# Output projection and final LayerNorm run from inside the attention loop, with the query blocks outermost

## The chip, the cores and the metric

The kernel runs on all 8 cores of one Trainium2 chip, one batch element per core, and every core executes the same program. The metric is the device time in microseconds of the slowest core. A core has a matrix engine (PE, with its weight loads listed as PEld), a vector engine (DVE), a scalar engine (ACT), GpSimd (POOL) and SyncE (SP). Each takes its instructions in the order of the program and stops at the first one whose semaphores are not there yet.

## The reference, cut to what matters

The layer gates two mixers, one of them softmax attention with 8 heads over 2048 latent queries and 2304 keys (256 context tokens and 2048 latents), concatenates them, projects to 1024 columns, and ends with a residual LayerNorm:

```
q  = rms_norm(q_a) @ w_qb              # (2048, 8 heads, 64+32), the last 32 rotated
kv = rms_norm(kv_a) @ w_kvb            # (2304, 8 heads, 64 key + 64 value)
p  = softmax((qn.kn + qr.kr) * scale)  # per head, 2048 x 2304
y_a = (p @ v) * silu(z_a)
y   = concat([y_a, y_b]) @ w_out
h_new = layer_norm(ALPHA * h + gate * y) * ln_g + ln_b      # h = layer_norm(x) * ln_in_g + ln_in_b
```

## The kernel before

The program is a list of operations, written in order. `P.add` (line 55) gives each a list of tile names that it reads and writes, works out from these names which earlier operations it has to wait for, and `flush` (line 126 on) puts each on its engine's queue with the waits. So the order in which the Python code emits operations is the order of every engine, and a tile name is all that decides a wait. A PSUM name (`psA0`, `psC`, ...) counts as written by whoever touches it, so matmuls into one bank and the reader of that bank alternate strictly.

The stages, in order: input LayerNorm and modulation; the mLSTM mixer, which fills `ycatT` rows 4 to 7; the attention inputs (`qnT`, `kvnT`, `szaT`, the rotary half of `Kh`); the attention loop (lines 882 to 975); and the output stage (lines 976 to 1064). `P.barrier()` separates them. `uT`, the modulated input, has no reader after the attention inputs.

**Attention loop.** `mainloop(h, pro)` takes one head and runs over four blocks of 512 queries; one (head, block) is called an iteration here, and there are 32. An iteration has 21 steps. Step s (below 18) issues the score matmul QK(s) into `psA[s % 3]` and its exponential on ACT into `PT[s % 4]`; from step 3 on it also issues PV(s-3), which adds to `psO` or `psE`. Two closures are left for the next iteration: `ep1` at its step 3 (reciprocal of the softmax sum by Ln and Exp on ACT, then a CAST and a subtraction on DVE into `rhl`) and `ep2` at its step 8 (two matmuls into `psB`, then `gg` and `ycatT` on DVE). `RECIP` and `RSQRT` are both Ln followed by Exp.

**Prologue.** `prologue(h + 1)` is a generator that makes the next head's keys, values and queries in 12 slots, one at each of steps 4, 10 and 16: five slots K0 to K4 (one matmul into `psC`, one CAST to `Kh`; K0 is 256 wide, the others 512), three slots V0 to V2 (8, 8 and 2 matmuls of 64 columns into `psD`, one CAST to `Vh`), four slots Q (two matmuls into `psC`, two into `psD`, four DVE operations). All evacuations are on DVE. Heads alternate between two `Kh`, `Vh` and `Qh` buffers.

**Output stage.** It starts after the barrier: `gate_bc` is built in 8 rounds of DVE, PE, ACT; four rows are loaded and broadcast to `rowsb`; `wout` is scaled by the gate in 8 DVE operations; then 16 tiles of 128 rows follow. A tile is 20 matmuls of 512 columns in two banks out of six (`bankset`), the residual add and statistics, RSQRT, two ACT normalisations, four DVE operations and a store. `xin` has three buffers, `pre` and `xo` two, and `stage1(lt + 1)`, the input side of the next tile, is issued ahead of tile lt's matmuls.

Helper lines: every matmul is recorded at line 234, ACT with a bias at 240, ACT without at 238, tensor_tensor at 249, tensor_scalar at 244, copies at 257 (ACT) and 259 (DVE).

Of the kernel before, what the change touches and what calls it, by code (L numbers as in the profile page):

```python
# [6 lines left out]
F32 = mybir.dt.float32  # L7
# [193 lines left out]
def build_nc(stage=99, dbg=None):  # L201
# [25 lines left out]
    def sbx(stack, name, shape, dt=F32):  # L227
        return stack.enter_context(nc.sbuf_tensor(name, list(shape), dt))
# [530 lines left out]
    if stage >= 3:  # L759
# [119 lines left out]
        MSET("dve", Vh[1][:], 0.0, w=[("Vh", 1)])  # L879
        MSET("dve", Vh[0][:, :, 64:65], 1.0, w=[("Vh", 0)])  # L880
        MSET("dve", Vh[1][:, :, 0:1], 1.0, w=[("Vh", 1)])
        def prologue(h):
            hb_ = h % 2
            voff = 0 if hb_ == 0 else 64
            for bi, (t0, N) in enumerate(blocks):
# [3 lines left out]
            for g0 in range(0, NT, 8):  # L889
# [4 lines left out]
                       r=["wkv", "kvnT"], w=["psD"])  # L894
                CP("dve", Vh[hb_][:, g0:g0 + nt_, voff:voff + 64], pv[:, 0:nt_, :], r=["psD"], w=[("Vh", hb_)])
                yield
            for qb in range(4):
                qs = slice(qb * 512, (qb + 1) * 512)
                for c in range(2):
                    MM(psC[0:96, :], wqA[:, c, h, :], qnT[:, c, qs], start=(c == 0), stop=(c == 1),  # L900
                       r=["wqA", ("qnT", c)], w=["psC"])
                for c in range(2):
                    MM(psD[0:96, :], wqB[:, c, h, :], qnT[:, c, qs], start=(c == 0), stop=(c == 1),
                       r=["wqB", ("qnT", c)], w=["psD"])
                CP("dve", Qh[hb_][0:64, qs], psC[0:64, :], r=["psC"], w=[("Qh", hb_, qb)])
                TT("dve", tmp_th[64:96, :], psC[64:96, :], rope[64:96, 0, qs], ALU.mult, r=["psC", "rope"],
                   w=["tmp_th"])
                TT("dve", tmp_zz[64:96, :], psD[64:96, :], rope[64:96, 1, qs], ALU.mult, r=["psD", "rope"],
                   w=["tmp_zz"])
                TT("dve", Qh[hb_][64:96, qs], tmp_th[64:96, :], tmp_zz[64:96, :], ALU.add,  # L910
                   r=["tmp_th", "tmp_zz"], w=[("Qh", hb_, qb)])
                yield

        pending = []

        def mainloop(h, pro):
            hb_ = h % 2
            M = 65 if hb_ == 0 else 128
            pd = 64 if hb_ == 0 else 0
            r0 = 0 if hb_ == 0 else 64  # L920
            for qb in range(4):
                qs = slice(qb * 512, (qb + 1) * 512)
                ob = (h * 4 + qb) % 2
                pso = psO if ob == 0 else psE
                pok = "psO" if ob == 0 else "psE"
                SK = 3
                for step in range(NT + SK):
# [6 lines left out]
                    if step >= SK:  # L934
                        kt = step - SK
                        MM(pso[0:M, :], Vh[hb_][:, kt, 0:M], PT[kt % 4][:], start=(kt == 0), stop=(kt == NT - 1),
                           r=[("Vh", hb_), ("PT", kt % 4)], w=[pok])
                    if pro is not None and step % 6 == 4:
                        next(pro, None)
                    if step == 3 and pending:  # L940
                        pending.pop(0)()
                    if step == 8 and pending:
# [33 lines left out]
    if stage >= 4:
        so = ExitStack()
        gate_bc = sbx(so, "gate_bc", [128, D])
        dg = sbx(so, "dg", [128, 128])
        for c in range(8):  # L980
            TS("dve", dg[:], ident_f[:], ada[:, 16 + c, 0:1], None, ALU.mult, r=["ident_f", ("ada", 2, 0)], w=["dg"])
            MM(psA[c % 2][:, 0:128], ones_f[:], dg[:], r=["ones_f", "dg"], w=["psA%d" % (c % 2)])
            CP("act", gate_bc[:, c * 128:(c + 1) * 128], psA[c % 2][:, 0:128], r=["psA%d" % (c % 2)], w=[("gate_bc", c)])
        rowsb = sbx(so, "rowsb", [128, 4, D])
        for a in range(4):
            DMA("sp", rowsb[:, a, :], rows_d[a:a + 1, :].partition_broadcast(128), w=[("rowsb", a)])
        xin = [sbx(so, "xin%d" % i, [128, D]) for i in range(3)]
        NPRE = 2
        for lt in range(NPRE):
            DMA("sp", xin[lt % 3][:], x_d[lt * 128:(lt + 1) * 128, :], w=[("xin", lt % 3)])  # L990
        for a in range(2):
            TS("dve", rowsb[:, a, :], rowsb[:, a, :], ALPHA, None, ALU.mult, r=[("rowsb", a)], w=[("rowsb", a)])
        for k in range(8):
            TT("dve", wout[:, k, :], wout[:, k, :], gate_bc[:], ALU.mult, r=["wout", "gate_bc"], w=[("wout", k)])
        bhl = sbx(so, "bhl", [1, 2, D], BF16)
        CP("dve", bhl[0:1, 0, :], rowsb[0:1, 1, :], r=[("rowsb", 1)], w=["bhl"])
        TT("dve", bhl[0:1, 1, :], rowsb[0:1, 1, :], bhl[0:1, 0, :], ALU.subtract, r=[("rowsb", 1), "bhl"], w=["bhl"])
        nmr = sbx(so, "nmr", [128, NT])
        STT("dve", nmr[:], stats[:, :, 0], -1.0, stats[:, :, 1], ALU.mult, ALU.mult, r=["stats"], w=["nmr"])
        nmo = sbx(so, "nmo", [128, 1])  # L1000
        xo = [sbx(so, "xo%d" % i, [128, D]) for i in range(2)]
        pre = [sbx(so, "pre%d" % i, [128, D]) for i in range(2)]
        st6o = sbx(so, "st6o", [128, 2, 6])
        mvo = sbx(so, "mvo", [128, 2])

        def prefetch(lt):
            if lt + NPRE < 16:
                nb = (lt + NPRE) % 3
                DMA("sp", xin[nb][:], x_d[(lt + NPRE) * 128:(lt + NPRE + 1) * 128, :], w=[("xin", nb)])

        def stage1(lt):
            xb = lt % 3
            ti = lt + 2
            ACT(xin[xb][:], xin[xb][:], AF.Identity, r=[("xin", xb), "nmr"], w=[("xin", xb)],
                scale=stats[:, ti, 1:2], bias=nmr[:, ti:ti + 1])
            TT("dve", xin[xb][:], xin[xb][:], rowsb[:, 0, :], ALU.mult, r=[("xin", xb), ("rowsb", 0)],
               w=[("xin", xb)])

        prefetch(0)
        stage1(0)  # L1020
        for lt in range(16):
            b = lt % 2
            xb = lt % 3
            cs = slice(lt * 128, (lt + 1) * 128)
            if lt + 1 < 16:
                stage1(lt + 1)
            bankset = [((psA[0], "psA0"), (psA[1], "psA1")), ((psA[2], "psA2"), (psO, "psO")),
                       ((psC, "psC"), (psD, "psD"))][lt % 3]
            for hf in range(2):
                hs = slice(hf * 512, (hf + 1) * 512)  # L1030
                pt_, pk_ = bankset[hf]
                for k in range(8):
                    MM(pt_[:], ycatT[:, k, cs], wout[:, k, hs], start=(k == 0), stop=False,
                       r=["ycatT", ("wout", k)], w=[pk_])
                for a in range(2):
                    MM(pt_[:], ones_b[0:1, :], bhl[0:1, a, hs], start=False, stop=(a == 1),
                       r=["ones_b", "bhl"], w=[pk_])
            for hf in range(2):
                hs = slice(hf * 512, (hf + 1) * 512)
                pt_, pk_ = bankset[hf]  # L1040
                TT("dve", pre[b][:, hs], pt_[:], xin[xb][:, hs], ALU.add, r=[pk_, ("xin", xb)],
                   w=[("pre", b, hf)])
                P.add("dve", lambda e, b=b, hf=hf, hs=hs: e.bn_stats(out=st6o[:, hf, :], in_=pre[b][:, hs]),  # L1043
                      r=[("pre", b, hf)], w=[("st6o", hf)])
            P.add("dve", lambda e: e.bn_aggr(out=mvo[:], in_=st6o[:]), r=["st6o"], w=["mvo"])  # L1045
            RSQRT(mvo[:, 1:2], mvo[:, 1:2], LN_EPS, r=["mvo"], w=["mvo"])
            STT("dve", nmo[:], mvo[:, 0:1], -1.0, mvo[:, 1:2], ALU.mult, ALU.mult, r=["mvo"], w=["nmo"])
            if lt + 1 < 16:
                prefetch(lt + 1)
            for hf in range(2):  # L1050
                hs = slice(hf * 512, (hf + 1) * 512)
                ACT(pre[b][:, hs], pre[b][:, hs], AF.Identity, r=[("pre", b, hf), "mvo", "nmo"], w=[("pre", b, hf)],
                    scale=mvo[:, 1:2], bias=nmo[:])
            for hf in range(2):
                hs = slice(hf * 512, (hf + 1) * 512)
                TT("dve", pre[b][:, hs], pre[b][:, hs], rowsb[:, 2, hs], ALU.mult, r=[("pre", b, hf), ("rowsb", 2)],
                   w=[("pre", b, hf)])
                TT("dve", xo[b][:, hs], pre[b][:, hs], rowsb[:, 3, hs], ALU.add, r=[("pre", b, hf), ("rowsb", 3)],
                   w=[("xo", b, hf)])
            DMA("pool", out_d[cs, :], xo[b][:], r=[("xo", b)], w=[("outd", lt)])  # L1060
        P.add("sp", lambda e: e.nop(), r=["outd"])
        P.barrier()
        so.close()
# [66 lines left out]
```

How the kernel before makes its waits and increments, by code:

```python
        def run(e):  # L146
            eng = eobj[e]
            seen = self.seen[e]
            for i in per[e]:
                op = ops[i]
                need = {}
                for d in op["deps"]:
                    dop = ops[d]
                    if (not dop["dma"]) and dop["eng"] == "pe" and e == "pe" and not op["dma"]:
                        continue
                    sem = dop["sem"]
                    key = id(sem)
                    if dop["val"] > need.get(key, (None, 0))[1]:
                        need[key] = (sem, dop["val"])
                for key, (sem, val) in need.items():
                    if seen.get(key, 0) >= val:
                        continue
                    eng.wait_ge(sem, val)
                    self.nwaits += 1
                    seen[key] = val
                ins = op["fn"](eng)
                if op["dma"]:
                    ins.then_inc(op["sem"], 16)
                elif op["sig"]:
                    ins.then_inc(op["sem"], 1)
                op["fn"] = None
```

## Time and profile before

| | us |
|---|---|
| median of the runs shown (1448.73 and 1452.82) | 1450.77 |
| the profiled execution | 1458.9 |
| its span on the slowest core (core 4) | 1457.1 |
| spans of the other cores | 1439.7 to 1456.9 |
| PE / DVE / ACT busy in the span | 906.9 / 753.7 / 842.5 |

The span runs from a core's first to its last instruction; the execution's own time is 1.8 us more. Busy time is the time in which an engine had an instruction under way. Matmuls overlap, so the busy time of one (about 0.38 us for 512 columns) is longer than the distance between two.

### The profile page before, as it was taken

To read this page: it belongs to the slowest core of one execution; us is meant where nothing else is said; L and a number is where in the kernel's file an instruction comes from. 1 tells how busy PE (TensorE), PEld (TensorE's weight loads), DVE (VectorE), ACT (ScalarE), POOL (GpSimd) and SP (SyncE) were. 2 spreads that over 40 slices of the span, in tenths; PEclk is the share of its full clock that TensorE was granted. 3 is DMA by queue.
4 is the path that set the end of the run, shared out by engine and by line. 5 is a ranking of instruction groups with operands and counts; after the bars stand their busy time and mean duration, and the time that the engine had idled before them with its cause. 6 is when DMAs were issued, how large, how long until landed. Compare 5 with 4: busy or idle time off the path is not lost. (4 is left out here: it accounts for less than half of the span.)

```text
span 1457.1 us, 18426 instructions; the slowest of 8 cores (1439.7 to 1457.1 us)
## 1 busy us (share of the span) xinstructions
PE 906.9 (62%) x5007; PEld 431.7 (30%) x5061; DVE 753.7 (52%) x1378; ACT 842.5 (58%) x1688; POOL 25.5 (2%) x40
## 2 busy tenths in 40 slices
PE   0113286466676554544229668888999988859770
PEld 0112142255543332323114323223333333213220
DVE  0267224456634655657625654455355345267776
ACT  0266324466656776667524428888877887813332
POOL 0000200000000000000000000000000000000000
PEclk9999996667687777776559959999888899957765
DMA  9742200000000000000040030000000000033331
GB/s 237 197 143 87 61 1 1 1 1 1 2 1 1 1 1 1 1 1 0 1 155 1 0 58 1 1 1 1 1 1 1 1 1 1 1 102 117 116 115 71
DMA packets 20308, 54.14 MB, mean 37 GB/s; under 512 B 4656, under 2 KB 6704, under 8 KB 20144
## 3 DMA queue, kind: packets, MB, share of 16 engines
q1 hardware_dynamic: 13232, 40.32, 8.9%
q0 software_dynamic: 6976, 12.63, 3.5%
q8 instruction: 45, 0.74, 0.2%
q14 instruction: 55, 0.45, 0.1%
HBM read 48.80 MB, written 8.39 MB: 39 GB/s over the span
## 5 line engine op out<-in xcount | busy, mean ns | idle before, releaser
L238 ACT ACTIVATE PT<-psA 128x512 bf16<-128x512 f32 x576 | 300.9, 601 | 71.4 <-PE psA L234 69.4
L234 PE MATMUL psA<-Qh,Kh 96*128 96x512 bf16 x576 | 226.7, 412 | 38.3 <-ACT PT L238 36.9
L234 PE MATMUL psO<-PT,Vh 128*65 128x512 bf16 (+1 forms) x280 | 111.7, 417 | 3.0 <-ACT PT L238 2.1
L234 PE MATMUL psE<-PT,Vh 128*65 128x512 bf16 (+1 forms) x281 | 109.4, 406 | 1.9 <-ACT PT L238 0.7
L234 PEld LDWEIGHTS psA<-Qh,Kh 96*128 96x128 bf16 x576 | 58.4, 101 | 169.6 <-issue 150.8
L259 DVE CAST rhl<-rden 1x512 bf16<-1x512 f32 x32 | 13.3, 416 | 131.6 <-ACT rden L238 131.6
L234 PE MATMUL psA<-wout,ycatT 128*128 128x512 bf16 x132 | 44.4, 486 | 17.8 <-DVE pre L249 10.0
L240 ACT ACTIVATE mvo<-mvo 128x1 f32<-128x1 f32 x16 | 3.2, 203 | 87.9 <-DVE mvo L1045 87.9
L234 PE MATMUL psA<-S0m,Vp 128*128 128x128 bf16 x128 | 26.1, 280 | 42.4 <-DVE S0m L249 42.4
L234 PE MATMUL psA<-uT,watt 128*128 128x512 bf16 (+3 forms) x127 | 28.7, 384 | 35.5 <-ACT wqA L257 35.5
L234 PE MATMUL psB<-scc,wadab 128*128 128x2 bf16 x192 | 5.5, 165 | 71.5 <-ACT wadab L257 68.0
L367 DVE BATCH_NORM_STATS2 st<-xt 128x6 f32<-128x512 f32 x36 | 23.0, 681 | 50.0 <-DMA xt<-ctx 41.3
L234 PE MATMUL psA<-uT,wxm 128*128 128x512 bf16 (+1 forms) x157 | 33.0, 374 | 23.9 <-DVE wxm L259 23.5
L238 ACT ACT_TABLE_LOAD x15 | 19.2, 1283 | 47.6 <-PE psA L234 38.8
L234 PE MATMUL psC<-Qd,KT 128*128 128x128 bf16 x128 | 15.9, 264 | 45.9 <-ACT KT L257 33.9
L252 DVE SCALAR_TENSOR_TENSOR state<-state,Ebc,dU 128x129 f32<-128x129 f32 x144 | 41.5, 348 | 4.9 <-ACT dU L238 4.4
L240 ACT ACT_TABLE_LOAD x11 | 14.1, 1283 | 50.0 <-DVE stats L259 43.8
L234 PE MATMUL psC<-xcT,wbd 128*128 128x128 bf16 (+2 forms) x133 | 17.7, 264 | 40.3 <-ACT wcol L238 37.8
L238 ACT ACTIVATE absd<-absd 128x512 f32<-128x512 f32 x64 | 40.3, 630 | 3.1
L234 PEld LDWEIGHTS psO<-PT,Vh 128*65 128x65 bf16 (+1 forms) x288 | 32.2, 112 | 30.5 <-issue 24.6
L259 DVE CAST Kh<-psC 64x512 bf16<-64x512 f32 (+1 forms) x40 | 25.1, 628 | 30.0 <-PE psC L234 29.3
L234 PEld LDWEIGHTS psE<-PT,Vh 128*65 128x65 bf16 (+1 forms) x288 | 31.4, 109 | 30.3 <-issue 23.6
(316 smaller groups left out, 2159.9 us busy)
## 6 DMA issues: line engine op xcount, KB each, us to landing
wada<-w_ada SPq DMA_DIRECT2D x3, 4096.0 KB, 22.1
xt<-x SPq DMA_DIRECT2D x16, 512.0 KB, 3.6
xin<-x SPq DMA_DIRECT2D x16, 512.0 KB, 4.5
out<-xo POOLq DMA_DIRECT2D x16, 512.0 KB, 3.0
win<-w_in SPq DMA_DIRECT2D x2, 1856.0 KB, 7.3
wxm<-w_in SPq DMA_DIRECT2D x2, 1024.0 KB, 7.4
wout<-w_out POOLq DMA_DIRECT2D x1, 2048.0 KB, 14.5
rowsb<-rows SPq DMA_DIRECT2D x4, 512.0 KB, 7.2
```

Source lines behind the costliest of these rows:

```text
L234: P.add("pe", lambda e: e.matmul(out, lhsT=lhsT, rhs=rhs, start=start, stop=stop), r=r, w=w)
L238: P.add("act", lambda e: e.activation(out=out, in_=in_, func=func, scale=scale), r=r, w=w)
L240: P.add("act", lambda e: e.activation(out=out, in_=in_, func=func, scale=scale, bias=bias), r=r, w=w)
L252: P.add(eng, lambda e: e.scalar_tensor_tensor(out=out, in0=in0, scalar=scalar, in1=in1, op0=op0, op1=op1), r=r, w=w)
L259: P.add(eng, lambda e: e.tensor_copy(out=out, in_=in_), r=r, w=w)
L367: P.add("dve", lambda e, b=b, hh=hh, s2=s2: e.bn_stats(out=st6[s2][:, hh, :], in_=xt[b][:, hh * 512:(hh + 1) * 512]), r=[("xt", b)], w=[(" ...
```

## The change

The attention loop is turned inside out: the outer loop runs over the four query blocks (`sb`), the inner over the 8 heads, and `mainloop` covers one block. The prologue of the next (head, block) makes all keys and values of that head again, and one query block. It has 9 slots, K0 to K4, V0 to V2 and one Q, taken at every even step.

The output stage becomes a generator, `outgen`. From the second block on (`allowed` is 0 in the first) it is advanced at steps 1, 4, 7, 10, 13, 16 and 19. It has 8 slots for the scaling of `wout` and then 17 for each tile; the projection is cut into quarters of 256 columns, which alternate between `psC` and `psD`. `pre` and `xo` have one buffer each instead of two, and all its large buffers lie in the memory of `uT`. What is left of it after the last iteration is run through at the end. The set-up (`gate_bc`, `rowsb`, `bhl`) stands ahead of the first prologue. The matmuls of the output read `("ycatT", 0)`, which covers every head and block.

```diff
-        def prologue(h):
+        def prologue(h, sb):
 ...
-            for qb in range(4):
+            for qb in range(sb * QSB, (sb + 1) * QSB):
 ...
-        def mainloop(h, pro):
+        def mainloop(h, sb, pro, og):
 ...
+            allowed = sb * TPS
-            for qb in range(4):
+            for qb in range(sb * QSB, (sb + 1) * QSB):
 ...
-                    if pro is not None and step % 6 == 4:
+                    if pro is not None and step % 2 == 0:
                         next(pro, None)
+                    if og is not None and step % 3 == 1 and out_state["tile"] < allowed:
+                        next(og, None)
 ...
+        def outgen():
+            for k in range(8):
+                TT("dve", wout[:, k, :], wout[:, k, :], gate_bc, ALU.mult, r=[("wout", k), "pre1"], w=[("wout", k)])
+                yield
+            for lt in range(16):
+                out_state["tile"] = lt
+                yield
...
+                for q in range(4):
+                    qs_ = slice(q * 256, (q + 1) * 256)
+                    pt_, pk_ = (psC, "psC") if q % 2 == 0 else (psD, "psD")
+                    for k in range(8):
+                        MM(pt_[:, 0:256], ycatT[:, k, cs], wout[:, k, qs_], start=(k == 0), stop=False,
+                           r=[("ycatT", 0) if k < 4 else ("ycatT", 1, lt), ("wout", k)], w=[pk_])
+                    for a in range(2):
+                        MM(pt_[:, 0:256], ones_b[0:1, :], bhl[0:1, a, qs_], start=False, stop=(a == 1),
+                           r=["ones_b", "bhl"], w=[pk_])
+                    TT("dve", pre1[:, qs_], pt_[:, 0:256], xin[xb][:, qs_], ALU.add, r=[pk_, ("xin", xb)],
+                       w=[("pre1", q)])
+                    yield
...
-        for _ in prologue(0):
+        og = outgen()
+        for _ in prologue(0, 0):
             pass
-        for h in range(8):
-            pro = prologue(h + 1) if h < 7 else None
-            mainloop(h, pro)
+        for sb in range(NSB):
+            for h in range(8):
+                if h < 7:
+                    pro = prologue(h + 1, sb)
+                elif sb + 1 < NSB:
+                    pro = prologue(0, sb + 1)
+                else:
+                    pro = None
+                mainloop(h, sb, pro, og)
...
         while pending:
             pending.pop(0)()
+        for _ in og:
+            pass
```

The 17 slots of a tile: one that only sets the tile's number; ACT and DVE on each half of `xin` (4); the four quarters (4); statistics (1); RSQRT (1); `nmo` (1); two ACT normalisations (2); two pairs of DVE operations of 512 columns (2); the store (1).

## Rows read from the trace of the kernel before

**Rows 1.** Spans and mean granted clock, two of the eight cores
```profile
core 0: 1445.1 us, clock 0.838
core 4: 1457.1 us, clock 0.801
```

**Rows 2.** Stage windows, core 4: PE, PEld, DVE, ACT, POOL busy (count), PEclk, DMA, GB/s
```profile
836.60:861.40 24.80, 11.40 (x39) 4.14 (x40) 17.10 (x25) 0.00 (x0) 0.90 (x1) 0.50 0.50 85
861.40:1273.40 412.00, 367.80 (x1473) 129.60 (x1486) 185.59 (x296) 336.04 (x639) 0.00 (x0) 0.89 0.00 1
1303.60:1457.10 153.50, 102.26 (x306) 29.99 (x312) 108.46 (x176) 49.01 (x80) 8.57 (x16) 0.67 0.28 100
```

**Rows 3.** Instruction groups by form, 780 to 1250 us: busy us, mean ns, idle before
```profile
L238 ACT ACTIVATE PT<-psA 128x512 bf16<-128x512 f32 x540 | 282.4, 601 | 68.6 <-PE psA L234 66.6 <-PE psO L234 0.9
...
L259 DVE CAST Kh<-psC 64x512 bf16<-64x512 f32 x32 | 21.8, 680 | 27.2 <-PE psC L234 26.6
...
L259 DVE CAST Vh<-psD 128x512 bf16<-128x512 f32 x16 | 11.0, 687 | 18.5 <-PE psD L234 18.3
...
L234 PE MATMUL psD<-wkv,kvnT 128*128 128x64 bf16 x144 | 9.0, 203 | 2.1 <-DVE Vh L259 2.1
```

**Rows 4.** Timeline of an iteration of the last head, no prologue: start, us, instruction
```profile
1238.60 0.81 PE L234 MATMUL psA<-Qh,Kh 96*128 96x512 bf16 x3
1239.13 2.06 ACT L238 ACTIVATE PT<-psA 128x512 bf16<-128x512 f32 x4 [0.89 <-PE psA L234]
...
1242.45 0.41 DVE L259 CAST rhl<-rden 1x512 bf16<-1x512 f32 x1 [9.01 <-ACT rden L238]
1242.96 0.68 DVE L249 TENSOR_TENSOR rhl<-rden,rhl 1x512 bf16<-1x512 f32 x1
...
1249.92 0.81 PE L234 MATMUL psA<-Qh,Kh 96*128 96x512 bf16 x3
```

**Rows 5.** Timeline of two key slots, at step 4 (K0) and step 10 (K1)
```profile
1176.67 0.30 PE L234 MATMUL psC<-kvnT,wkv 128*64 128x256 bf16 x1
...
1179.46 0.42 DVE L259 CAST Kh<-psC 64x256 bf16<-64x256 f32 x1
...
1181.26 0.40 PE L234 MATMUL psC<-kvnT,wkv 128*64 128x512 bf16 x1
...
1181.99 0.68 DVE L259 CAST Kh<-psC 64x512 bf16<-64x512 f32 x1
```

**Rows 6.** Timeline of a query slot at step 16 and the next iteration's start
```profile
1104.46 0.70 PE L234 MATMUL psC<-qnT,wqA 128*96 128x512 bf16 x2
...
1105.27 0.68 DVE L259 CAST Qh<-psC 64x512 bf16<-64x512 f32 x1 [2.88 <-PE psC L234]
...
1107.04 0.96 PE L234 MATMUL psA<-Qh,Kh 96*128 96x512 bf16 x3
...
1107.45 0.68 DVE L249 TENSOR_TENSOR Qh<-tmp_th,tmp_zz 32x512 bf16<-32x512 f32 x1
```

**Rows 7.** Timeline of the first prologue, before the loop
```profile
841.67 0.42 DVE L259 CAST Kh<-psC 64x256 bf16<-64x256 f32 x1
...
854.52 0.68 DVE L249 TENSOR_TENSOR Qh<-tmp_th,tmp_zz 32x512 bf16<-32x512 f32 x1
...
861.47 1.49 PE L234 MATMUL psA<-Qh,Kh 96*128 96x512 bf16 x3
```

**Rows 8.** Timeline of the output stage's opening
```profile
1279.52 1.77 SPq L273 DMA_DIRECT2D rowsb<-rows  x4
1279.58 0.29 DVE L244 TENSOR_SCALAR dg<-ident_f,ada 128x128 f32<-128x128 f32 x1 [0.70 <-PEq L173]
...
1289.59 1.29 DVE L244 TENSOR_SCALAR rowsb<-rowsb 128x1024 f32<-128x1024 f32 x2
...
1291.07 10.53 DVE L249 TENSOR_TENSOR wout<-wout,gate_bc 128x1024 bf16<-128x1024 bf16 x8 [0.19 <-ACT gate_bc L257]
```

**Rows 9.** Instruction groups by form, 1245 to 1457 us
```profile
L234 PE MATMUL psA<-wout,ycatT 128*128 128x512 bf16 x132 | 44.4, 486 | 17.8 <-DVE pre L249 10.0 <-DVE wout L249 7.6 <-issue 0.2
L240 ACT ACTIVATE pre<-pre,nmo,mvo 128x512 f32<-128x512 f32 x32 | 24.3, 806 | 6.5 <-DVE nmo L252 6.5
```

**Rows 10.** Chain that ended last: the normalisation of tiles 0 and 15
```profile
1312.06 0.82 ACT pre L240
...
1447.14 0.82 ACT pre L240
```

More of the change, by code:

```diff
@@ L881, in build_nc @@
         MSET("dve", Vh[1][:, :, 0:1], 1.0, w=[("Vh", 1)])
-        def prologue(h):
+        NSB = 4
+        QSB = 4 // NSB
+        TPS = 16 // NSB
+        uTf = uT[:].rearrange("p c t -> p (c t)").bitcast(F32)
+        rowsb = uTf[:, 0:4096].rearrange("p (a n) -> p a n", n=D)
+        xin = [uTf[:, 4096 + i * 1024:4096 + (i + 1) * 1024] for i in range(3)]
+        xo1 = uTf[:, 7168:8192]
+        pre1 = uTf[:, 8192:9216]
+        gate_bc = pre1
+        dg = sbx(sa, "dg", [128, 128])
+        bhl = sbx(sa, "bhl", [1, 2, D], BF16)
@@ new lines, in build_nc @@
+        nmr = sbx(sa, "nmr", [128, NT])
+        nmo = sbx(sa, "nmo", [128, 1])
+        st6o = sbx(sa, "st6o", [128, 2, 6])
+        mvo = sbx(sa, "mvo", [128, 2])
+        NPRE = 2
+        for a in range(4):
+            DMA("sp", rowsb[:, a, :], rows_d[a:a + 1, :].partition_broadcast(128), w=[("rowsb", a)])
+        for lt in range(NPRE):
+            DMA("sp", xin[lt % 3], x_d[lt * 128:(lt + 1) * 128, :], w=[("xin", lt % 3)])
+        for a in range(2):
+            TS("dve", rowsb[:, a, :], rowsb[:, a, :], ALPHA, None, ALU.mult, r=[("rowsb", a)], w=[("rowsb", a)])
@@ new lines, in build_nc @@
+        CP("dve", bhl[0:1, 0, :], rowsb[0:1, 1, :], r=[("rowsb", 1)], w=["bhl"])
+        TT("dve", bhl[0:1, 1, :], rowsb[0:1, 1, :], bhl[0:1, 0, :], ALU.subtract, r=[("rowsb", 1), "bhl"], w=["bhl"])
+        STT("dve", nmr[:], stats[:, :, 0], -1.0, stats[:, :, 1], ALU.mult, ALU.mult, r=["stats"], w=["nmr"])
+        for c in range(8):
+            TS("dve", dg[:], ident_f[:], ada[:, 16 + c, 0:1], None, ALU.mult, r=["ident_f", ("ada", 2, 0)], w=["dg"])
+            MM(psA[c % 2][:, 0:128], ones_f[:], dg[:], r=["ones_f", "dg"], w=["psA%d" % (c % 2)])
+            CP("act", gate_bc[:, c * 128:(c + 1) * 128], psA[c % 2][:, 0:128], r=["psA%d" % (c % 2)], w=[("pre1", c)])
@@ L914, in build_nc @@
         pending = []
-        def mainloop(h, pro):
+        blk_cnt = [0]
+        def mainloop(h, sb, pro, og):
             hb_ = h % 2
@@ L920, in mainloop @@
             r0 = 0 if hb_ == 0 else 64
-            for qb in range(4):
+            allowed = sb * TPS
+            for qb in range(sb * QSB, (sb + 1) * QSB):
                 qs = slice(qb * 512, (qb + 1) * 512)
-                ob = (h * 4 + qb) % 2
+                ob = blk_cnt[0] % 2
+                blk_cnt[0] += 1
                 pso = psO if ob == 0 else psE
@@ L961, in mainloop @@
                 pending.append(ep2)
-        for _ in prologue(0):
-            pass
-        for h in range(8):
-            pro = prologue(h + 1) if h < 7 else None
-            mainloop(h, pro)
-            if pro is not None:
-                for _ in pro:
-                    pass
+        og = outgen()
+        for _ in prologue(0, 0):
+            pass
+        for sb in range(NSB):
[7 more added lines that the diff above has]
+                mainloop(h, sb, pro, og)
+                if pro is not None:
+                    for _ in pro:
+                        pass
@@ L971, in build_nc @@
         while pending:
             pending.pop(0)()
+        for _ in og:
+            pass
+        P.add("sp", lambda e: e.nop(), r=["outd"])
         P.barrier()
         sa.close()
[L976 to L1063, printed above, removed]
```

41 lines of the change are left out of this document (added).

## The prediction, made before the changed kernel was run

> **What bounds the kernel now.** First the spans and clocks of all cores: core 4 is the slowest, about 12 us behind core 0 [rows 1]. Then the windows by stage. The attention loop takes 412 of the 1457 us, with PE busy 368, ACT 336 and DVE only 186; the output tiles take another 153.5, with DVE busy 108 and PE and ACT not full [rows 2]. On the face of it the loop has DVE time to spare and the output stage needs mostly DVE, and this is what the change draws on.
>
> Third, one iteration without a prologue. From its first QK to the next iteration's first QK is 1249.92 - 1238.60 = 11.32 us [rows 4]. In it ACT has 18 exponentials, four in 2.06 us, so 0.51 apart, plus Ln and Exp of ep1; with 0.89 idle at the start [rows 4] that is the iteration: ACT sets it. PE needs less: three matmuls in 0.81 us of which the last is some 0.38 long make 0.215 for 512 columns, and 38 of them 8.2 us. This stretch has the granted clock 1.0, the 2.4 GHz level; over the loop core 4 had 0.89 [rows 2]. The mean iteration is 412 / 32 = 12.9.
>
> Fourth, what a wait of PE costs. PE is in order, so when it stands at a prologue matmul, no later QK is issued, and ACT has at most the three scores in `psA` left, 1.5 us. Hence the prologue's chain through `psC`, `psD` and DVE decides, and the sum of busy times doesn't. In the kernel before, slots are six steps (some 3 us) apart, and this chain is always done in time.
>
> **The price of a slot, from rows.** A key slot: matmul at 1181.26, CAST from 1181.99 for 0.68 [rows 5]; with 0.07 until PE sees it, the next matmul into `psC` can start 1.5 us after this one. Slots will now be two steps apart, 1.03 us at ACT's pace. A slot at step 4: its CAST waits on DVE behind the `rhl` pair of ep1, which waits for ACT: matmul at 1176.67, CAST at 1179.46, 2.8 us later [rows 5]. The pair ends 1243.64 - 1238.60 = 5.0 us after the iteration's first QK [rows 4]. A value slot of eight matmuls: 144 took 9.0 us, so 0.5 for eight, and a CAST of 0.69 [rows 3]. A query slot: matmul at 1104.46, last DVE operation over at 1107.45 + 0.68, 3.7 us later [rows 6]. Before, `Qh` was written at least an iteration ahead; now Q is at step 16 and the next iteration's first QK needs it. In the same rows that QK came 2.6 us after the slot's matmul.
>
> **An iteration of the first block (no output work), time zero at its first QK.** K0 is cast at 1.3. K1 (step 2) at 1.35, cast done 2.8. K2 (step 4) at 2.85, but its CAST waits for the `rhl` pair until 5.1 and ends at 5.8. K3 (step 6) can't start before 5.9: PE stands there for some 2.5 us and ACT runs dry. K3 done 7.3; K4 (step 8) 7.4 to 8.8; then ep2 puts `gg` and `ycatT` on DVE, 8.9 to 10.4. V0's CAST follows, until 11.2; V1 12.6; V2 (two matmuls) 13.4. Q starts at 13.7, as steps 15 and 16 come first, and `Qh` is ready 3.7 later, at 17.4. Iteration: **17.5 us**. The same walk without slots gives 11.4 against the 11.32 of the row, so I trust it within a microsecond or so. Bounds: 12.4, if all slots are covered and ACT and PE alone count (PE: 8.2 + keys 4.5 x 0.215 + values 18 x 0.0625 + queries 4 x 0.215 = 11.2), and 20, if PE's share falls to the lower clock.
>
> **An iteration of the other blocks.** 7 output slots each, 56 in a block, 168 in all. 8 go to `wout`, 160 to tiles of 17 slots: 9.4 tiles are done in the loop, 6.6 are left. The guard `allowed` never stops it. One tile takes 17 / 7 = 2.43 iterations. Its four quarters each take a turn of `psC` or `psD`: ten matmuls of 256 columns at 0.108 = 1.1, latency 0.4, an add of about 0.42 (the 256-wide CAST of rows 5), 0.1 to be seen: 2.0. Four are 8.0 per tile, 3.3 per iteration. The quarters also read `("ycatT", 0)`, so one at step 10 waits for ep2's last DVE operation as well. The other DVE work: a tile had 108.5 / 16 = 6.8 us [rows 2]; quarters and half-width `xin` add 0.45, so 7.25, less the four adds 5.6, or 2.3 per iteration. ACT has 49.0 / 16 = 3.1 per tile, 1.3 per iteration [rows 2]. Of these 3.6 some fall where DVE and ACT now stand idle; I count 1.7. Iteration: 17.5 + 3.3 + 1.7 = **22.5 us**. The `wout` slots (10.5 us [rows 8]) are inside this. Bounds: 14 (DVE's sum: (185.6 + 24 x 4.8) / 32 = 9.4, plus 3.3 of output, and gaps), and 26 at the lower clock.
>
> 24 x 4.8 is the recomputed keys and values: 24 passes more, each 4 x 0.68 + 0.42 + 2 x 0.69 + 0.29 of DVE. On PE they are 24 x 2.1 = 50 us.
>
> **Set-up.** The DMAs of `rowsb`, `xin` and `wout` are issued together near 837. `rowsb` was used 10 us after its issue [rows 8]; `wout` now competes, so DVE, in order, waits until 847 or later; row operations 3.4; gate rounds 11 (1279.58 to the scaling at 1291.07, less the rows' 1.3 beside it [rows 8]); then the prologue with one query block, 854.52 + 0.68 - 841.67 = 13.5 [rows 7]. First QK at 875.4 instead of 861.47: **+14** (bounds +8 and +30).
>
> **Tail.** ep1 and ep2 take 6 us as before. A left-over tile: before, 15 intervals from 1312.06 to 1447.14 are 9.0 each [rows 10], DVE 6.8 and 2.2 of waits for ACT and the statistics. Now DVE 7.25, the same 2.2, and for quarters 2 and 3 it waits on PE, which may only start when quarter 0's bank is free: together 1.7 (2.4 GHz) to 3.9 (1.2 GHz), take 2.6. That is 12 a tile, 80 for 6.6, and 5 for the last store: 91.
>
> **Sum.** 861.4 + 14 + 8 x 17.5 + 24 x 22.5 + 91 = 1646 span, 1648 for the execution (1.8 more). The profiled execution was 1458.9 where the median is 1450.8, a factor 0.9944: **1639 us**, 13% slower. What is saved in the output stage (184 us from 1273.4 to the end become 91) is less than the 268 by which the loop grows.
>
> A rule that bears on this: the Trainium skill, "Perfetto Trace Analysis", section on matmuls, says that independent matmul groups should rotate through PSUM banks so that one group's evacuation overlaps the next group's matmuls. The kernel before gives the output six banks; the change puts keys, values, queries and output on two. Applied here, the rule speaks against the change and would give what the walk gives.
>
> **Rivals.**
> *Cover works, faster.* DVE is idle 226 of the loop's 412 us [rows 2], and if the queues shift against each other so that no slot stands in PE's way, iterations come down to 12.4 and 14: 861.4 + 14 + 99 + 336 + 91 = 1401, **1395 us**. For it: DVE's idle time is that large. Against: K2 to K3, where the row shows 2.8 us with nothing of the change in it [rows 5]. The same page of the Trainium skill, section on optimization strategy, says that interleaving regimes with different contended engines may improve performance; by that rule this rival would hold.
> *Slots cost only their PE time.* If chains of `psC` and `psD` are absorbed but PE's work, ACT's work and the late `Qh` are not: 11.3 + 3.0 = 14.3 with `Qh` hardly late, and 14.3 + 1.8 + 1.3 = 17.4 minus what ACT's idle absorbs, 16.9: 861.4 + 14 + 114 + 406 + 91 = 1486, **1480 us**, at the edge of 2%.
> *The clock falls too.* PE's columns fill 13 of 22.5 us (58%), where before they filled about 9.4 of 12.9. The output tiles, at 4.3 of 9.0, had the granted clock 0.67 [rows 2]. If the loop gets that, a query or output slot's matmuls take up to double: iterations of 20 and 26, 861.4 + 14 + 160 + 624 + 91 = 1750, **1742 us**.
> *The interleaving gives less than said:* that 6.6 of 16 tiles stay behind is in all sums.
>
> **How the numbers follow.** Forecast 0.68, the clock 0.12, PE time only 0.12, cover works 0.08. About 2% is what a measurement of this kernel tells from no change. Faster by over 2%: 0.07; within 2%: 0.08 (the edge of the third case and some of the fourth); slower: 0.85. Range 1510 to 1740: above the third case, to the lower-clock case, one tenth outside at either end.
>
> **What would show it.** First QK near 875; first-block iterations of 16 to 19 us, later ones of 20 to 25; long waits PE `psC` <- DVE `Kh` and PE `psA` <- DVE `Qh` that hardly exist today; ACT idle in the loop several times today's 69 us [rows 3] for PE; 160 `Kh` CASTs instead of 40; 6 to 7 tiles behind the loop at 11 to 13 us each. Wrong: iterations below 15, or no wait of PE for DVE at the key slots. The tail's PE (486 ns a matmul) and ACT (806 ns) rows [rows 9] should stay at half and equal size.

## The result and the profile after

The changed kernel took 1697.85 us (median), the one before 1451.5. Some executions of either kernel ran in a slower state of the chip, so the ratio, 1.1669 with a 95% interval of 1.1624 to 1.1713, goes by the others alone (median 1692.5 for the changed kernel), which makes it 242 us slower where the two medians differ by 246. The forecast was 1639, range 1510 to 1740. The direction and the place of the loss were right; 59 us were missing. The profiled execution took 1685.2 us, with a span of 1683.4 on core 5.

First the windows by stage of the changed kernel, core 5 (length, then busy us and count of PE, PEld, DVE, ACT, POOL, then the granted clock, DMA share, GB/s). The four are set-up, first block, the other three blocks, and the tail behind the loop:

```profile
837.00:882.00 45.00, 18.06 (x57) 7.69 (x57) 22.51 (x38) 7.95 (x17) 0.90 (x1) 0.51 0.55 128
882.00:1018.00 136.00, 112.68 (x512) 40.90 (x512) 76.08 (x123) 85.47 (x156) 0.00 (x0) 0.89 0.00 1
1018.00:1563.00 545.00, 445.37 (x1908) 170.33 (x1905) 303.16 (x509) 296.31 (x535) 4.84 (x9) 0.79 0.05 18
...
1570.00:1683.40 113.40, 51.68 (x252) 26.77 (x250) 49.32 (x94) 23.32 (x40) 3.73 (x7) 0.62 0.14 51
```

ACT was busy 336 of 412 us in the loop before [rows 2]; now it is busy 85 of 136 in the first block. DVE isn't full either, 76 of 136. No engine but PE looks busy, and PE's own count says little: a matmul is listed with 0.38 us where two are 0.215 apart. That is the look of a chain that goes from engine to engine. Where its links are, the waits of 882 to 1563 us say (total us, times, longest):

```profile
ACT PT L238 <- PE psA L234: 280.8, 258, 4.6
...
DVE Kh L259 <- PE psC L234: 77.0, 92, 2.0
...
DVE Vh L259 <- PE psD L234: 55.7, 69, 1.8
PE psC L234 <- DVE Kh L259: 54.0, 45, 3.4
DVE rhl L259 <- ACT rden L238: 52.2, 31, 2.6
...
PE psA L234 <- DVE Qh L249: 28.5, 24, 1.3
...
PE psD L234 <- DVE Vh L259: 12.6, 17, 1.5
```

ACT waited 66.6 us for scores before [rows 3] and waits 281 now. PE waits for DVE's evacuation of `psC`, and for `Qh`, neither of which limited the loop before. And DVE in turn waits for PE: each key slot is a turn of one, then the other.

The timeline of one first-block iteration (core 5) shows both places where the forecast's walk had PE wait:

```profile
950.87 0.64 PE L234 MATMUL psC<-kvnT,wkv 128*64 128x512 bf16 x1
...
951.76 0.41 DVE L259 CAST rhl<-rden 1x512 bf16<-1x512 f32 x1 [1.45 <-ACT rden L238]
...
952.28 0.68 DVE L249 TENSOR_TENSOR rhl<-rden,rhl 1x512 bf16<-1x512 f32 x1
...
952.89 0.67 DVE L259 CAST Kh<-psC 64x512 bf16<-64x512 f32 x1
...
953.70 0.38 PE L234 MATMUL psC<-kvnT,wkv 128*64 128x512 bf16 x1 [0.38 <-DVE Kh L259]
...
961.11 0.59 PE L234 MATMUL psC<-qnT,wqA 128*96 128x512 bf16 x2
...
964.00 0.68 DVE L249 TENSOR_TENSOR Qh<-tmp_th,tmp_zz 32x512 bf16<-32x512 f32 x1
964.82 0.38 PE L234 MATMUL psA<-Qh,Kh 96*128 96x512 bf16 x1 [1.20 <-DVE Qh L249]
```

K2's matmul is at 950.87, its CAST starts 2.0 later, behind the `rhl` pair, and K3's matmul 0.14 after the CAST's end. The iteration that began at 947.80 ends at 964.82, with the first QK waiting 1.20 us for `Qh`. That is 17.02 us; the walk gave 17.5. K2's CAST ends 5.76 us after the iteration's start and K3's matmul starts at 5.90; the walk said 5.8 and 5.9. But PE itself is idle for only 0.38 us there, not for 2.5: the matmuls before K3 are 0.43 us apart, with a granted clock of 0.53 from 949.8 to 953.4 us, so PE spends the time on them. The dates of this chain are set by ACT and DVE, and here a slower PE hides in it; in the long iterations of experiment 1 it no longer does.

Not every iteration is like this one. Over the first block (seven intervals between `rhl` CASTs) the mean is 17.7 to 17.8 us on four cores, this one among them, and 18.3 to 20.1 on the other four.

The ledger against the kernel before, in spans:

| part | before | after | difference | forecast |
|---|---|---|---|---|
| stage start (first MEMSET of `Vh`) | 837.1 | 842.4 | +5.3 | 0 |
| set-up and first prologue, to the first QK | 24.4 | 33.5 | +9 | +14 |
| attention loop | 412 | 687 | +275 | +268 |
| behind the loop | 183.7 | 120.4 | -63 | -93 |
| span | 1457.1 | 1683.4 | +226 | +189 |

Two rows need care. The stage starts anywhere from 837.1 to 843.4 us on cores 0 to 5 before, and from 834.8 to 843.6 on the eight cores after; core 5 has 841.8 and 842.4. So the +5.3 is the spread of the cores and no effect of the change. And core 4 before had a lower clock for part of the loop (last section): from its first QK to its last `rhl` CAST it took 413.5 us, where cores 0 to 3, 6 and 7 took 395 to 399. Against those the loop grew by about 290 us.

In the three later blocks, 23 iterations lie between two `rhl` CASTs at 1019.99 and 1548.77 us: 23.0 each, where 22.5 was forecast (21.9 to 23.0 over the cores). Single ones take 17.5 to 30.8 us, so 22.5 was right for their mean and for none in particular.

### The profile page after: what moved, and what is told of

The parts are those of the page before. It is cut to its first block and busy times, and to the rows that moved or that the text cites. A ratio compares the mean times of both kernels' runs of the same rounds, so it can differ in the third digit from the quotient of the medians.

```text
span 1683.4 us, 20959 instructions; the slowest of 8 cores (1658.7 to 1683.4 us)
## 1 busy us (share of the span) xinstructions
PE 1054.4 (63%) x5933; PEld 511.5 (30%) x5933; DVE 874.6 (52%) x1618; ACT 866.2 (51%) x1703; POOL 25.5 (2%) x40
## 5 line engine op out<-in xcount | busy, mean ns | idle before, releaser
L259 DVE CAST Kh<-psC 64x512 bf16<-64x512 f32 (+1 forms) x160 | 100.4, 628 | 88.6 <-PE psC L234 86.1
L234 PE MATMUL psE<-PT,Vh 128*128 128x512 bf16 x288 | 128.0, 464 | 2.8 <-ACT PT L238 2.8
L234 PE MATMUL psO<-PT,Vh 128*65 128x512 bf16 x288 | 127.8, 463 | 2.9 <-ACT PT L238 2.9
L234 PE MATMUL psC<-kvnT,wkv 128*64 128x512 bf16 (+1 forms) x160 | 71.6, 447 | 53.4 <-DVE Kh L259 45.9
L234 PE MATMUL psC<-wout,ycatT 128*128 128x256 bf16 x256 | 47.9, 351 | 64.2 <-DVE uT L249 46.7
L259 DVE CAST Vh<-psD 128x512 bf16<-128x512 f32 (+1 forms) x96 | 53.3, 555 | 57.4 <-PE psD L234 57.2
L249 DVE TENSOR_TENSOR uT<-uT 128x512 f32<-128x512 f32 x96 | 65.7, 689 | 28.1 <-ACT uT L240 22.4
L234 PE MATMUL psD<-wout,ycatT 128*128 128x256 bf16 x256 | 44.6, 333 | 9.7 <-DVE tmp_zz L249 5.7
L234 PE MATMUL psD<-wkv,kvnT 128*128 128x64 bf16 x576 | 40.8, 218 | 12.4 <-DVE Vh L259 10.7
L234 PEld LDWEIGHTS psO<-PT,Vh 128*65 128x65 bf16 x288 | 38.0, 132 | 33.9 <-issue 21.9
## 6 DMA issues: line engine op xcount, KB each, us to landing
wout<-w_out POOLq DMA_DIRECT2D x1, 2048.0 KB, 25.9
```

The source lines that it names most:

```text
L234: P.add("pe", lambda e: e.matmul(out, lhsT=lhsT, rhs=rhs, start=start, stop=stop), r=r, w=w)
L249: P.add(eng, lambda e: e.tensor_tensor(out=out, in0=in0, in1=in1, op=op), r=r, w=w)
L259: P.add(eng, lambda e: e.tensor_copy(out=out, in_=in_), r=r, w=w)
```

## Experiments

All ratios are against the kernel before, run on the same chip.

**1. The reordering alone.** The kernel before with the block loop outermost, and nothing of the output stage touched:

```diff
-        for h in range(8):
-            pro = prologue(h + 1) if h < 7 else None
-            mainloop(h, pro)
+        for sb in range(4):
+            for h in range(8):
+                pro = prologue(h + 1, sb)   # or prologue(0, sb + 1)
+                mainloop(h, sb, pro)        # one block; slots at step % 2 == 0
```

> The kernel before with its output stage untouched; only the attention loop is turned inside out (query block outermost, one block per head, keys and values made again in each, 9 prologue slots at the even steps). Theory of the slot chain (PE stands at a slot until DVE has emptied psC or psD): all 32 iterations take the 17.0 us that the first block of the changed kernel shows, first QK some 9 us earlier than before (one query slot instead of four in the first prologue), 853 + 32 x 17.1 + 6 + 178 = 1584 span, about 1577. If only the PE time of the added matmuls counted (14.3 per iteration): about 1487. If DVE's idle time covered it (12.4): about 1434.

Measured: 1631.86 us, ratio 1.1252 (1.1223 to 1.1281). So the reordering alone costs 181 of the 242 us, and neither "DVE's idle time covers it" (1434) nor "only the PE time counts" (1487) comes near. But it is 55 us above what 17.1 us an iteration would give. These are four of the `rhl` CASTs, one per iteration, on its core 2:

```profile
1127.10 0.41 DVE L259 CAST rhl<-rden 1x512 bf16<-1x512 f32 x1 [1.45 <-ACT rden L238]
1144.26 0.42 DVE L259 CAST rhl<-rden 1x512 bf16<-1x512 f32 x1 [1.59 <-ACT rden L238]
1164.66 0.41 DVE L259 CAST rhl<-rden 1x512 bf16<-1x512 f32 x1 [1.45 <-ACT rden L238]
1181.82 0.42 DVE L259 CAST rhl<-rden 1x512 bf16<-1x512 f32 x1 [1.59 <-ACT rden L238]
```

Iterations of the same instructions take 17.2 or 20.4 us. The mean of the 30 between 880.08 and 1433.08 is 18.4, and 32 x 1.3 = 42 us of the 55. The two lengths alternate here as the heads do with their two sets of buffers, but it isn't the buffers: in the first block of the changed kernel, core 5 has five short ones in a row and core 7 five long ones. What differs is the clock. Core 7's windows over two long iterations and a short one:

```profile
939.70:960.20 20.50, 16.89 (x63) 5.99 (x64) 9.95 (x17) 11.35 (x21) 0.00 (x0) 0.71 0.00 1
960.20:980.70 20.50, 18.35 (x67) 6.49 (x66) 9.85 (x16) 11.26 (x21) 0.00 (x0) 0.67 0.00 0
1001.20:1018.30 17.10, 14.19 (x69) 5.20 (x67) 9.90 (x17) 10.96 (x21) 0.00 (x0) 0.95 0.00 1
```

The long ones have the granted clock 0.71 and 0.67, the short one 0.95: more or less of the iteration at 1.2 instead of 2.4 GHz, while DVE's busy time is the same and ACT's nearly so. Which comes first, the stall or the clock, these rows don't tell. The rival "the clock falls too" was therefore partly true. The loop didn't sink to the lower clock as a whole, but was a mixture, and the 17.5 of the forecast was right for one of its two lengths.

**2. The late query.** The query slot is taken first, the same work in another order:

```diff
+            for qb in range(sb * QSB, (sb + 1) * QSB):    # query slot, now ahead of the key slots
+                ...
             for bi, (t0, N) in enumerate(blocks):
```

> The changed kernel with the query slot taken first (step 0) instead of last (step 16); no work is added or removed. Theory of the chain with a late Qh as its last link: the next iteration's first QK no longer waits for Qh, and a first-block iteration falls from 17.0 to about 15.3 us, the others by 1 to 2: 45 to 60 us less than the changed kernel, about 1640. If the chain is only shifted and the key and value slots end as late as Qh did: under 15 us less.

Measured: 1659.04 us, ratio 1.1435 (1.1404 to 1.1465), 34 us less than the changed kernel by the ratios. It lies between the two. The wait PE <- `Qh` of 1.20 us times 31 iterations is 37 us: the visible wait went and nothing more. The rest of the chain was only shifted, and PE now waited 61.8 us for `Kh` (core 7, 882 to 1563 us) instead of 53.5 to 59.2.

**3. The repetition of keys and values.**

```diff
-            for bi, (t0, N) in enumerate(blocks):
+            for bi, (t0, N) in enumerate(blocks if sb == 0 else []):
```
and the same for the value slots.

> The changed kernel without the key and value slots in the blocks after the first; the attention of those blocks then reads the keys and values of the last two heads, so this part of the computation is left out. Theory of the chain: 24 iterations fall from 23.0 to about 16.5 us (11.4 bare, 3.3 for the quarters' turns of psC and psD, 1.7 for the rest), 155 us less than the changed kernel, about 1540. If only their PE time counts: 24 x 2.1 = 50 less. If their DVE time counts: 24 x 4.8 = 115 less.

Measured: 1534.48 us, ratio 1.0596 (1.055 to 1.0642), 156 us less by the ratios where the chain gave 155. The PE time of these matmuls (50) or their DVE time (115) falls well short. Each repeated pass cost 6.5 us, of which PE worked 2.1.

**4. Tile names.**

```diff
-                    ACT(pre1[:, hs], ..., r=["pre1", "mvo", "nmo"], ...
+                    ACT(pre1[:, hs], ..., r=[("pre1", 2 * hf), ("pre1", 2 * hf + 1), "mvo", "nmo"], ...
```
and likewise `("xin", xb, hf)` for `("xin", xb)`, and for the DVE operations on `pre1`.

> The changed kernel with the tile names of the output tile narrowed to the half that an instruction really touches (xin, pre1). The theory for the tail's 16 us a tile: 1 us is DVE waiting for both ACT normalisations instead of one, another 1 to 2 us are the second half of xin waiting on ACT, which waited for DVE's work on the first half. Expected: 16.0 to about 14 us a tile in the tail, 10 to 20 us less in all, the loop nearly unchanged. If the tail's tile is set by the matmuls of quarters 2 and 3 alone, no change.

Measured: 1667.35 us, ratio 1.1499 (1.1477 to 1.1521), 25 us less. This is a tile of the changed kernel's tail, whose store is the POOL row; the tile before was stored at 1581.46:

```profile
1583.95 1.86 PE L234 MATMUL psC<-wout,ycatT 128*128 128x256 bf16 x8 [7.88 <-DVE uT L249]
...
1586.45 0.43 DVE L249 TENSOR_TENSOR uT<-psC,uT 128x256 f32<-128x256 f32 x1 [2.32 <-PE psC L234]
...
1588.59 0.42 DVE L249 TENSOR_TENSOR uT<-psD,uT 128x256 f32<-128x256 f32 x1 [1.71 <-PE psD L234]
...
1593.54 3.68 DVE L249 TENSOR_TENSOR uT<-uT 128x512 f32<-128x512 f32 x5 [1.97 <-ACT uT L240]
...
1597.24 0.53 POOL L273 DMA_DIRECT2D out<-uT  x1 [15.24 <-DVE uT L249]
1597.37 0.81 ACT L240 ACTIVATE uT<-uT,nmr,stats 128x512 f32<-128x512 f32 x1 [3.23 <-DVE uT L249]
1598.29 0.69 DVE L249 TENSOR_TENSOR uT<-uT 128x512 f32<-128x512 f32 x1 [1.07 <-ACT uT L240]
```

A tile takes 15.8 to 16.1 us. DVE waits 4.0 of them (2.32 + 1.71) for quarters 2 and 3, whose matmuls started only after quarter 0's bank was free, at the lower clock (the eight of quarter 2 take 1.86 us, those of the next tile's quarter 0 take 1.05). It waits 1.97 for both halves of ACT's normalisation, where one would do. The last two rows are the other name: ACT's work on the second half of `xin` reads the name of the whole, so it waited 3.23 us for DVE, and DVE then waited 1.07 for it. With narrow names the stores of the tail come 13.4 us apart:

```profile
1618.37 0.53 POOL L273 DMA_DIRECT2D out<-uT  x1 [13.11 <-DVE uT L249]
1631.67 0.53 POOL L273 DMA_DIRECT2D out<-uT  x1 [12.77 <-DVE uT L249]
1645.22 0.53 POOL L273 DMA_DIRECT2D out<-uT  x1 [13.02 <-DVE uT L249]
```

2.6 us for 6.6 tiles are 17 us, nearly the whole difference of the two spans (1683.4 and 1664.9); no row here accounts for the other 8 of the 25. So the names are the tail's first mis-sized term, and the quarters' 4.0 instead of 2.6 the second.

**5. Banks.** Key and value slots alternate between `psC` and `psD`:

```diff
-                MM(psC[0:64, 0:N], wkv[:, h, 0:64], ...
+                pk, pkk = (psC, "psC") if bi % 2 == 0 else (psD, "psD")
+                MM(pk[0:64, 0:N], wkv[:, h, 0:64], ...
```

> The changed kernel with the key and value slots alternating between psC and psD (K0, K2, K4, V1 in psC, K1, K3, V0, V2 in psD) instead of five in a row in psC and three in psD. Same instructions otherwise. Theory of the chain: a slot then waits for the evacuation two slots back; the walk gives 14.4 instead of 17.0 us for a first-block iteration (K3 no longer waits for K2, Q waits for V1 and V2), 1.5 to 2.6 us for each of the 32: 50 to 85 us less than the changed kernel, about 1630. If DVE's own queue sets the pace and PE's waits only move: under 20 us less.

Measured: 1587.78 us, ratio 1.0953 (1.093 to 1.0976), 104 us less, more than the upper end. First-block iterations are 14.6 to 15.2 us long (14.4 expected). What the expectation left out is the clock, which is higher here. Its windows, core 3, first block and the rest:

```profile
882.00:1000.00 118.00, 101.04 (x516) 38.53 (x514) 80.36 (x128) 84.87 (x161) 0.00 (x0) 0.97 0.00 1
1000.00:1460.00 460.00, 372.60 (x1864) 145.96 (x1863) 293.06 (x499) 279.86 (x522) 5.04 (x9) 0.92 0.06 21
```

0.97 and 0.92 stand against 0.89 and 0.79 on core 5 of the changed kernel, and no iteration of this first block takes 20 us any more. Nothing but bank names was changed, so the DVE queue's length was not what set the pace. The Trainium skill's rule in "Perfetto Trace Analysis" (matmuls rotate through banks) is confirmed here at 104 us for 32 iterations.

**6 and 7. Two outer blocks, crowded and spaced.** `NSB = 2`, with the prologue's ten slots at every second step or at every fourth:

```diff
-        NSB = 4
+        NSB = 2
...
-                    if pro is not None and step % 2 == 0:
+                    if pro is not None and step % 4 == 0:      # spaced run only
```

> The changed kernel with NSB = 2 (two outer blocks of 1024 queries, so keys and values are made twice per head and not four times) and the prologue's 10 slots at every fourth step. 112 output slots in the loop: 6.1 tiles inside, 9.9 behind it. Theory: slots 2.1 us apart are longer than the 1.5 us of one psC turn, so hardly any stall; 16 iterations of about 13 and 16 of about 18 us, 496 instead of 687, and a tail of 170 instead of 120: about 1550. If the stalls came from the number of waits between the engines and not from their spacing, the loop stays above 600: 1650.

Measured: 1569.0 us, ratio 1.0822 (1.0803 to 1.084); 19 us above the expectation. Iterations of the first half take mostly 12.8 to 13.7, as expected; those of the second half, with output slots, 13 to 24 (18.6 in the mean, from 1102.18 to 1380.77 in 15).

> Two outer blocks with the prologue's slots at every second step, so the ten slots of a head crowd into the first of its two iterations. Same work as the spaced run (1569). Theory of the chain: the first iteration takes 17 as in the changed kernel, the second 11.5 to 12, 28.5 to 29 a pair where spacing gave 26.8: with 16 pairs 30 to 50 us more than the spaced run, about 1610. If only the number of slots matters: 1569.

Measured: 1599.22 us, ratio 1.1034 (1.0987 to 1.1082), 31 us more than spaced for the same work. In the first half, a pair of iterations is 19.1 to 20.5 and 11.4 to 11.8 us (17 and 11.5 to 12 expected), where the spaced run has 12.8 to 13.7 for each. In this pair of runs, spacing and not count is what stalls.

**8. Only the opening in the loop.** The kernel before, with 29 slots for `rowsb`, `bhl`, `nmr`, `gate_bc` and the scaling of `wout`:

```diff
+                    if h >= 1 and step in (13, 19):
+                        next(su, None)
```

> The kernel before (heads outermost), with only the opening of its output stage put into the attention loop: rowsb, bhl, nmr, gate_bc and the scaling of wout in 29 slots at steps 13 and 19 of the heads from 1 on, buffers in the memory of uT; the 16 tiles stay behind the loop. DVE is idle 226 of 412 us there and these slots are far from the prologue's. Theory: the 24 us between the loop and the first tile go, the slots cost 3 to 8 us: about 1432, ratio 0.987. If any work put into the loop costs its own time, as in the changed kernel: no change.

Measured: 1439.25 us, ratio 0.9922 (0.9904 to 0.994): 11 us less, not 19. That is clear of 1.0, but under the 2% that the forecast took for a change. The 24 us are gone: the first output matmul starts 1.6 us after the start of the last `ycatT` (core 5), and the first store is at 1296.92, where it was at 1316.55 before.

```profile
1279.13 0.69 DVE L249 TENSOR_TENSOR ycatT<-psE,gg 64x512 bf16<-64x512 f32 x1
1280.59 0.33 SPq L273 DMA_DIRECT2D uT<-x  x1
1280.59 1.28 ACT L240 ACT_TABLE_LOAD   x1 [4.40 <-PEq L173]
1280.72 3.57 PE L234 MATMUL psA<-wout,ycatT 128*128 128x512 bf16 x8 [2.50 <-PEq L173]
```

But 24 less 11 leaves 13 us that the slots must cost, more than the 3 to 8 I had allowed. The traces find about 8 of them in the loop: from first QK to last `rhl` CAST it takes 399 to 402 us on cores 0 to 3 and 409 to 410 on cores 4 to 7, in the mean 405, where six cores took 397 before. DVE's idle time hides part of a slot, not all.

**9. What a tile costs inside.** Keys made once, and no output slot in the loop (`allowed = 0`), to be held against experiment 3:

> Keys and values made in the first block only (that part of the later blocks' attention is left out, they read the last two heads' keys and values), and no output slot is taken in the loop: all 16 tiles come behind it. Against the run without the keys' repetition it gives the price of 9.4 tiles inside the loop. Theory: iterations of the later blocks 12.3 instead of 16.5 us, so 24 x 4.2 = 100 us for 9.4 tiles, about 11 us a tile, more than the 9.0 that a tile takes in the stage of the kernel before; tail 16 x 16 = 256; about 1600. If the interleaving hides a tile's DVE work: 12.3 becomes 15 or more here, too.

Measured: 1592.33 us, ratio 1.0983 (1.0953 to 1.1014). The `rhl` CASTs at both ends of 24 iterations, first without the interleaving, core 1:

```profile
1011.78 0.42 DVE L259 CAST rhl<-rden 1x512 bf16<-1x512 f32 x1 [0.78 <-ACT rden L238]
...
1309.71 0.42 DVE L259 CAST rhl<-rden 1x512 bf16<-1x512 f32 x1 [7.72 <-ACT rden L238]
```

and with it (experiment 3, core 6):

```profile
1010.59 0.42 DVE L259 CAST rhl<-rden 1x512 bf16<-1x512 f32 x1 [0.78 <-ACT rden L238]
...
1394.19 0.42 DVE L259 CAST rhl<-rden 1x512 bf16<-1x512 f32 x1 [4.94 <-ACT rden L238]
```

12.4 against 16.0 us an iteration: 86 us for 9.4 tiles and the scaling of `wout`, or 9.1 a tile with its share of the scaling. Behind the loop, the kernel before takes 9.0 a tile, and the scaling 10.5 once, together 95, or 10.1 a tile with its share. So even with the keys' repetition taken out, moving 9.4 tiles into the loop saves 9 us by this sum, while the 6.6 tiles behind it cost 7 us more each (16 instead of 9). The likely reason for so small a gain, not tested by itself: a tile needs 4.3 us of PE and 3.1 of ACT, and these two bound the loop; only its DVE work finds room.

**10. Three repairs at once** (banks, names, query first):

> The changed kernel with three repairs at once: alternating banks (alone 110 us less), narrow tile names (30 less) and the query slot first (37 less). Theory: the late Qh and the bank turns are links of one chain, so they add up only partly, the tail's part adds fully: 1540 to 1550, still 6 to 7% slower than the kernel before, because what is left (keys and values made four times, PE and ACT time of the tiles in a loop that PE and ACT bound) is no stall. If stalls were all of it: 1451 or less.

Measured: 1552.35 us, ratio 1.0706 (1.0675 to 1.0736), 140 us less, where the single ones add up to 163. First-block iterations are 14.0 to 14.3 us. That is close to 11.3 bare and 3.0 of PE time for nine slots, but not all stalls are gone. In seven of these iterations (core 6, 888 to 987 us) PE waits for DVE:

```profile
PE psC L234 <- DVE tmp_th L249: 6.0, 7, 0.9
...
PE psD L234 <- DVE Kh L259: 2.3, 7, 0.4
```

That is 1.2 us an iteration; K0 now meets the query slot in `psC`. 102 us remain. Iterations of the later blocks take 18.8 us in the mean on most cores, 4.7 more than those of the first: 113 us for 9.4 tiles and the scaling of `wout`, where the kernel before needs 95 behind the loop. So with banks and names repaired, and the keys made every time, tiles inside cost more than outside.

**11. The repairs with two blocks:**

> The three repairs with two outer blocks and slots at every fourth step. Against the spaced run with two blocks (1569): the tail's 9.9 tiles at 2 to 3 us less each, 25, and 10 to 20 less in the loop's second half: about 1530. It would beat the kernel before only if interleaved tiles cost clearly less than the 9.0 us they take behind the loop; the pair of runs with keys made once gave 9.1.

Measured: 1533.99 us, ratio 1.0577 (1.0538 to 1.0616), as expected. No interleaved version came near the kernel before.

**12. The opening in the loop, and a filled wait.** The tiles of experiment 8, with `xin`'s multiplication moved:

```diff
             RSQRT(mvo[:, 1:2], mvo[:, 1:2], LN_EPS, r=["mvo"], w=["mvo"])
+            if lt + 1 < 16:
+                stage1b(lt + 1)          # TT("dve", xin[xb], xin[xb], rowsb[:, 0, :], ...)
             STT("dve", nmo[:], ...
```

> The run with the set-up in the loop of the kernel before, and in its 16 tiles the next tile's 1.2 us multiplication of xin moved on DVE to the place where DVE waits 0.7 us for RSQRT (between the statistics and nmo). Theory: DVE bounds these tiles, with 2.2 us of waits in 9.0; 0.7 of the wait is filled, ACT's normalisation starts 0.6 later: 0.2 to 0.7 us a tile, 3 to 11 us less than that run, 1428 to 1436. If ACT's late start outweighs it: up to 8 us more.

Measured: 1427.07 us, ratio 0.9844 (0.9814 to 0.9874), 1.6% less than the kernel before and the best of all, though under 2% too. It is just below the expectation. The 1.2 us operation now lies where DVE waited for RSQRT:

```profile
1297.73 0.21 DVE L1065 BATCH_NORM_AGGREGATE mvo<-st6o 128x2 f32<-128x12 f32 x1
1297.86 1.20 DVE L249 TENSOR_TENSOR uT<-uT 128x1024 f32<-128x1024 f32 x1
1298.03 0.20 ACT L240 ACTIVATE mvo<-mvo 128x1 f32<-128x1 f32 x1 [4.34 <-DVE mvo L1065]
1298.33 0.20 ACT L238 ACTIVATE mvo<-mvo 128x1 f32<-128x1 f32 x1
1298.97 0.15 DVE L252 SCALAR_TENSOR_TENSOR nmo<-mvo 128x1 f32<-128x1 f32 x1
```

The stores come 8.3 us apart (1303.63, 1311.89, 1320.12 us), not 9.1 as in experiment 8.

## Why the prediction was right, and where it was off

Of the 59 us that were missing, 37 are in the span (+5 where the stage starts, -5 in the set-up, +7 in the loop, +30 behind it) and 22 in the step from the profiled execution to the median.

- *The chain through `psC`, `psD` and DVE decides, not the busy times.* Right. Walk 17.5, measured 17.0 in the short kind of iteration; the walk's dates stand in the timeline within about 0.5 us; banks alone take 104 us off (experiment 5), spacing 31 (experiments 6 and 7). Its one wrong detail is PE's wait before K3, 2.5 in the walk and 0.38 in the iteration shown. From DVE's end to PE's next matmul 0.14 us pass (K3 above), not the walk's 0.07; a turn of `psC` is 1.5 us with either.
- *The price of keys and values four times.* Right in kind: a repeated pass costs its slots' turns and not its 2.1 us of PE. Experiment 3 measured 156 us, 6.5 a pass. With the queries' late slot and the repetition together the reordering costs 181 (experiment 1).
- *Other blocks 22.5 us.* Measured 23.0 on the profiled core. The 9.4 tiles inside: the stores fit, seven come in the tail. That the whole loop came within 7 us of the forecast is in part luck: the walk is for a constant clock, and the short and long iterations mixed as they did.
- *Set-up +14.* Measured +9. DVE started on the rows at 847.0, 4.6 after the stage's first MEMSET, and waited only 0.61 us for the second one, where I had put 10; `wout`, landing in 25.9 us, didn't hold them up.
- *The tail, 12 us a tile.* This is the step of the sum that was most mis-sized: 16.0 a tile, which makes 26 of the 29 us that the part behind the loop took beyond the forecast. I took over the 2.2 us of waits of the tile before, though the names had become coarser (experiment 4: 2.6 us), and put the quarters at 2.6, between 1.7 and 3.9, where 4.0 was at the slow end.
- *The clock left out of the sum.* I kept it as a rival of 0.12, all or nothing. The runs show a mixture of iterations at 17 and 20.4 us, which differs by core and execution. On the profiled core's first block it happened to be mild.
- *The factor from the profiled execution to the median.* I took 0.9944 over from the kernel before; here it was 1.0075 (1697.85 / 1685.2), 22 us of the 59. The factor only says which execution the profiler happened to catch: before, one with a lower clock on cores 4 and 5, here the second fastest of twelve. It should not have been carried over.
- *Rival "cover works".* It fell: DVE was idle in both kernels, and its idle time was never the scarce thing. The Trainium skill's rule in "Perfetto Trace Analysis", section on optimization strategy, speaks for regimes with different contended engines; here PE and ACT were needed by both, and even with free keys the gain was 9 us by the sum of experiment 9.
- *Rival "slots cost only their PE time".* False for the changed kernel. Experiment 10 comes to 14.1 us in the first block, near this rival's 14.3, but with 1.2 us of PE's waits for DVE still in it, so the agreement is not a proof.

## What to carry to other kernels

Before work is put into a loop, count for each slot how long its PSUM bank is taken (matmul, wait in the evacuating engine's queue, evacuation) and compare that with the distance between slots. If it is longer, the in-order matmul engine stands at the slot and every engine behind it starves, whatever the busy shares promise. And ask whether the moved work needs the loop's own bounding engines: here, with a tile's share of the `wout` scaling, it cost 9.1 us inside at best (keys not repeated) and 10.1 outside, and reordering the loop to make the move possible cost 181 us. Only the stage's opening was worth moving.

## What the runs showed of the hardware that I had not expected

A loop of identical iterations can fall into two lengths, 17.1 and 20.4 us, with granted clocks of 0.95 and about 0.7, on one core within 80 us. It looks as if a small stall could so cost more than its own length, and its removal give more: experiment 5 gained 3.3 us an iteration where the walk, at a constant clock, had 2.6 at most. No run changes the clock alone, so this is a reading and not shown.

And cores 4 and 5 of the kernel before were granted 0.81 for 168 us of the loop, between the two levels, while cores 6 and 7 of the same die had 0.99. The windows of cores 4 and 0:

```profile
1008.00:1176.00 168.00, 156.39 (x597) 56.20 (x603) 83.00 (x132) 132.50 (x252) 0.00 (x0) 0.81 0.00 1
...
1008.00:1176.00 168.00, 147.33 (x641) 50.95 (x641) 89.04 (x142) 139.54 (x271) 0.00 (x0) 0.99 0.00 1
```

Core 4's iterations there took 12.7 to 14.4 us; core 0's took 11.6 to 13.6.
